# Last row blocks of an encoder layer: scalings on ScalarE and GpSimd, residual and weighting one step earlier

## The reference, cut to what matters

```python
h = _rmsnorm(x, norm_g[l]);  proj = h @ w_in[l]        # u, v, gates, q, k, v, ...
mix = jnp.concatenate([ya * silu(ga), yb * silu(gb), yc * silu(gc)], axis=-1)
x = x + jnp.einsum('bse,ed->bsd', mix, w_out[l])       # (1024, 2048)
...
y = x32 * lax.rsqrt(jnp.mean(x32 * x32, axis=-1, keepdims=True) + EPS)
return y * final_g
```

## Time and profile before

| | |
|---|---|
| median of 3 runs | 1252.67 us (1252.62 to 1253.96) |
| the profiled execution | 1252.9 us |
| its span, first to last instruction | 1251.1 us |
| granted TensorE clock | 0.997 of full speed |
| TensorE busy | 1230.0 us (98%) |
| VectorE busy | 831.2 us (66%) |
| ScalarE busy | 498.8 us (40%) |
| GpSimd busy | 54.9 us (4%) |

### The profile page before, as it was taken

One profiled execution on the slowest core, in us unless ns is written; L12 is line 12 of the kernel. 1 busy time (PEld: TensorE's weight loads), 2 busy tenths in 40 slices (PEclk: granted clock), 3 DMA queues, 4 the chain that ended last, 5 costly groups with the idle time before them and its releaser, 6 DMA issues.

```text
span 1251.1 us, 16376 instructions
## 1 busy us (share of the span) xinstructions
PE 1230.0 (98%) x6310; PEld 1014.3 (81%) x6310; DVE 831.2 (66%) x1115; ACT 498.8 (40%) x887; POOL 54.9 (4%) x70
## 2 busy tenths in 40 slices
PE   7999999999999999999999999999999999999996
PEld 6878888888988888888888887888888888888884
DVE  7657666664576577776376568777678755665556
ACT  7435454435553354454334112333333512323135
POOL 3400000003110000000000000000000000000000
PEclk9999999999999999999999999999999999999998
DMA  8499446353655256565896877659999799855769
GB/s 312 128 311 332 146 163 210 141 184 124 220 189 211 102 182 222 185 216 201 335 343 225 322 299 270 214 189 356 415 350 354 296 351 395 305 202 204 284 223 332
DMA packets 98813, 314.16 MB, mean 251 GB/s; under 512 B 10128, under 2 KB 13232, under 8 KB 87344
## 3 DMA queue, kind: packets, MB, share of 16 engines
q1 hardware_dynamic: 98736, 313.12, 69.2%
HBM read 241.77 MB, written 71.30 MB: 250 GB/s over the span
## 4 chain that ended last, share of the span: by engine, by line
PE 95%; DMA 2%; DVE 1%; ACT 1%; issue 1%; SPq 0%; ACTq 0%; DVEq 0%
PE n_bank L1561 17%; PE n_bank L1563 17%; PE n_bank L1562 17%; PE t_bank L1561 11%; PE t_bank L1562 10%; PE t_bank L1563 10%; PE e_bank L1561 2%; PE n_bank L1756 2%; PE e_bank L1563 2%; PE e_bank L1562 2%; PE n_bank L1782 2%; PE n_bank L1766 1%; DMA raw<-w_dram 1%; PE e_bank L1796 1%; PE e_bank L1806 1%
## 5 line engine op out<-in xcount | busy, mean ns | idle before, releaser
L1106 DVE TENSOR_TENSOR w_lo<-raw,w_hi 128x1024 fp32r<-128x1024 f32 (+1 forms) x116 | 138.0, 1228 | 153.2 <-ACT w_hi L812 152.9
L1561 PE MATMUL t_bank<-op_hi,w_hi 128*128 128x512 f32 x512 | 203.1, 397 | 0.0
L1562 PE MATMUL t_bank<-op_lo,w_hi 128*128 128x512 f32 x512 | 199.7, 390 | 0.0
L1563 PE MATMUL t_bank<-op_hi,w_lo 128*128 128x512 f32 x512 | 199.4, 389 | 0.0
L812 ACT ACTIVATE w_hi<-raw 128x1024 fp32r<-128x1024 f32 (+1 forms) x116 | 113.2, 1021 | 167.1 <-PE t_bank L1563 111.5
L1561 PE MATMUL n_bank<-s_ring,w_hi 128*128 128x512 f32 x448 | 178.0, 397 | 0.0
L1563 PE MATMUL n_bank<-s_ring,w_lo 128*128 128x512 f32 x448 | 174.4, 389 | 0.0
L1562 PE MATMUL n_bank<-s_ring,w_hi 128*128 128x512 f32 x448 | 174.3, 389 | 0.0
L1561 PE MATMUL n_bank<-w_hi,s_ring 128*128 128x512 f32 x448 | 174.3, 389 | 0.0
L1562 PE MATMUL n_bank<-w_lo,s_ring 128*128 128x512 f32 x448 | 174.3, 389 | 0.0
L1563 PE MATMUL n_bank<-w_hi,s_ring 128*128 128x512 f32 x448 | 174.3, 389 | 0.0
(11 more groups left out here) (225 smaller groups left out, 1825.7 us busy)
## 6 DMA issues: line engine op xcount, KB each, us to landing
s_ring<-x_parts SPq DMA_DIRECT2D x112, 512.0 KB, 6.1
s_ring<-m_parts SPq DMA_DIRECT2D x112, 512.0 KB, 6.0
raw<-w_dram SPq DMA_DIRECT2D x46, 1024.0 KB, 5.1
y_w<-w_b_dram SPq DMA_DIRECT2D x16, 1024.0 KB, 11.2
mix<-x_t_dram SPq DMA_DIRECT2D x56, 256.0 KB, 5.0
m_parts<-stage SPq DMA_DIRECT2D x24, 512.0 KB, 7.6
x_parts<-stage SPq DMA_DIRECT2D x32, 256.0 KB, 3.0
x_parts<-mix SPq DMA_DIRECT2D x32, 256.0 KB, 3.0
```

Of the source, the lines that this page charges most:

```text
L1106: ve.tensor_tensor(w_lo[:, J % 2, part], w_source(J)[:, part], w_hi[:, J % 2, part].bitcast(F32), ALU.subtract).then_inc(lo_done, 1)
L1561: pe.matmul(psum_out, stat[0], mov[0], start=first, stop=False)
L1562: pe.matmul(psum_out, stat[0], mov[1], start=False, stop=False)
L1563: return pe.matmul(psum_out, stat[1], mov[0], start=False, stop=last)
```

## The change

In the first half, y11[3] is scaled by ScalarE as a third block behind y11[2] and y12[2], and y12[3] by GpSimd; so y12[3] gets a `weigh` of its own, at step(3, 10). VectorE's part there shrinks to sum and inverse (`first_root`). In pair 3 the residual of y21[3] is added at step 12, not 13; in VectorE's program this stands ahead of `first_root`, and the last `weigh` (y22[3]) comes right behind `first_root`. In the second half GpSimd scales y22[2], ScalarE y21[2] only. In the last loop VectorE's addition of tile 3 stands ahead of its scalings of tile 2. The stores keep their order; their waits name the new semaphores.

```diff
...
         ssq_done, y_weighed, ssq_summed = sem("ssq_done"), sem("y_weighed"), sem("ssq_summed")
         y_root, y_inverted = sem("y_root"), sem("y_inverted")
         y_scaled, y_normed, y_stored = sem("y_scaled"), sem("y_normed"), sem("y_stored")
+        first_normed, second_scaled = sem("first_normed"), sem("second_scaled")
         dve_settled, pool_settled = sem("dve_settled"), sem("pool_settled")
         def w_source(J):
...
                 if n == CHUNKS - 2:
                     for c, y, done, count in ((0, y11[2], y_scaled, 4), (1, y12[2], y_scaled, 8),
-                                              (2, y11[3], y_normed, 4), (3, y12[3], y_normed, 8)):
+                                              (2, y11[3], y_scaled, 12), (3, y12[3], first_normed, 4)):
                         sp.wait_ge(done, count)
                         sp.dma_start(out[0:HS, 512 * c:512 * c + 512].rearrange("(t r) d -> r t d", t=ST), y[:]
                                      ).then_inc(y_stored, 16)
             for st in range(ST):
                 s0 = HS + P * st
-                for c, y, done, count in ((3, y22[3], y_normed, 8 + 2 * st + 1), (0, y21[2], y_scaled, 8 + 2 * st + 1),
-                                          (2, y21[3], y_normed, 8 + 2 * st + 2), (1, y22[2], y_scaled, 8 + 2 * st + 2)):
+                for c, y, done, count in ((3, y22[3], y_normed, 2 * st + 1), (0, y21[2], y_scaled, 12 + st + 1),
+                                          (2, y21[3], y_normed, 2 * st + 2), (1, y22[2], second_scaled, st + 1)):
                     sp.wait_ge(done, count)
                     sp.dma_start(out[s0:s0 + P, 512 * c:512 * c + 512], y[:, st, :]).then_inc(y_stored, 16)
             sp.wait_ge(y_stored, 16 * (4 + 4 * ST))
...
                                      sink_sb[:, 2 * (n // 2):2 * (n // 2) + 2].unsqueeze(2).broadcast_to([P, 2, 2])
                                      ).then_inc(sink_set, 1)
+            pool.wait_ge(y_inverted, 1)
+            pool.wait_ge(y_weighed, 6)
+            for st in range(ST):
+                tile = y12[3][:, st, :]
+                pool.tensor_scalar(tile, tile, rstd_y[0][:, st:st + 1], None, ALU.mult).then_inc(first_normed, 1)
+            for st in range(ST):
+                tile = y22[2][:, st, :]
+                pool.wait_ge(y_inverted, 2 + st)
+                pool.tensor_scalar(tile, tile, rstd_y[1][:, st:st + 1], None, ALU.mult).then_inc(second_scaled, 1)
         @block.scalar
         def _(sc):
...
                 sc.activation(root_y[0][:], ssq_sum[0][:], ACT.Sqrt, bias=eps_sb[:], scale=1.0 / D
                               ).then_inc(y_root, 1)
                 sc.wait_ge(y_inverted, 1)
-                for y, weighed in ((y11[2], 1), (y12[2], 2)):
+                for y, weighed in ((y11[2], 1), (y12[2], 2), (y11[3], 5)):
                     sc.wait_ge(y_weighed, weighed)
                     for st in range(ST):
                         tile = y[:, st, :]
                         sc.activation(tile, tile, ACT.Copy, scale=rstd_y[0][:, st:st + 1]).then_inc(y_scaled, 1)
-            def finish_second(st):
+            def second_root(st):
                 col = slice(st, st + 1)
                 sc.wait_ge(ssq_summed, 2 + st)
                 sc.activation(root_y[1][:, col], ssq_sum[1][:, col], ACT.Sqrt, bias=eps_sb[:], scale=1.0 / D
                               ).then_inc(y_root, 1)
+            def second_scale(st):
+                tile = y21[2][:, st, :]
                 sc.wait_ge(y_inverted, 2 + st)
                 sc.wait_ge(y_weighed, 4)
-                for y in (y21[2], y22[2]):
-                    tile = y[:, st, :]
-                    sc.activation(tile, tile, ACT.Copy, scale=rstd_y[1][:, col]).then_inc(y_scaled, 1)
+                sc.activation(tile, tile, ACT.Copy, scale=rstd_y[1][:, st:st + 1]).then_inc(y_scaled, 1)
+            def last_square(st):
+                sc.wait_ge(res_added, 6)
+                sc.wait_ge(y_added, added(PAIRS - 1, Q_A22, st))
+                square_y(1, 2, y21[3], st)
             def split_hi(J, parts=(0, 1)):
                 for part in parts:
...
                     copy_u(p, range(ST - 1))
                 if J == step(PAIR_O + 1, 12):
                     finish_first()
-            for st in range(ST):
-                sc.wait_ge(res_added, 6)
-                sc.wait_ge(y_added, added(PAIRS - 1, Q_A22, st))
-                square_y(1, 2, y21[3], st)
-                finish_second(st)
+            for st in range(ST - 2):
+                last_square(st)
+                second_root(st)
+                second_scale(st)
+            last_square(ST - 2)
+            second_root(ST - 2)
+            second_scale(ST - 2)
+            last_square(ST - 1)
+            second_root(ST - 1)
+            second_scale(ST - 1)
         @block.vector
...
             def weigh(i):
-                y, c, n = ((y11[2], 0, 1), (y12[2], 1, 2), (y22[2], 1, 3), (y21[2], 0, 4), (y11[3], 2, 5), (y22[3], 3, 7))[i]
+                y, c, n = ((y11[2], 0, 1), (y12[2], 1, 2), (y22[2], 1, 3), (y21[2], 0, 4), (y11[3], 2, 5), (y12[3], 3, 6), (y22[3], 3, 7))[i]
                 ve.wait_ge(ssq_done, ST * n)
                 ve.wait_ge(final_g_loaded, 16)
                 ve.tensor_tensor(y[:], y[:], final_g_sb[:, 512 * c:512 * c + 512].unsqueeze(1).broadcast_to([P, ST, 512]),
...
                                             ALU.subtract)
                 last.then_inc(pool_in, 1)
-            def finish_first():
+            def first_root():
                 ve.wait_ge(ssq_done, 6 * ST)
                 ve.tensor_reduce(ssq_sum[0][:], ssq[0][:], AX.X, ALU.add).then_inc(ssq_summed, 1)
                 ve.wait_ge(y_root, 1)
                 ve.reciprocal(rstd_y[0][:], root_y[0][:]).then_inc(y_inverted, 1)
-                ve.wait_ge(y_inverted, 1)
-                ve.wait_ge(y_weighed, 5)
-                for st in range(ST):
-                    tile = y11[3][:, st, :]
-                    ve.tensor_scalar(tile, tile, rstd_y[0][:, st:st + 1], None, ALU.mult).then_inc(y_normed, 1)
-                for st in range(ST):
-                    tile = y12[3][:, st, :]
-                    ve.scalar_tensor_tensor(out=tile, in0=tile, scalar=rstd_y[0][:, st:st + 1],
-                                            in1=final_g_sb[:, 1536:2048], op0=ALU.mult, op1=ALU.mult
-                                            ).then_inc(y_normed, 1)
-            def finish_second(st):
+            def second_root(st):
                 ve.wait_ge(ssq_done, 7 * ST + st + 1)
                 ve.tensor_reduce(ssq_sum[1][:, st:st + 1], ssq[1][:, st, :], AX.X, ALU.add).then_inc(ssq_summed, 1)
                 ve.wait_ge(y_root, 2 + st)
                 ve.reciprocal(rstd_y[1][:, st:st + 1], root_y[1][:, st:st + 1]).then_inc(y_inverted, 1)
+            def second_norm(st):
+                y, z = y22[3], y21[3]
                 ve.wait_ge(y_inverted, 2 + st)
-                ve.wait_ge(y_weighed, 6)
-                tile = y22[3][:, st, :]
-                ve.tensor_scalar(tile, tile, rstd_y[1][:, st:st + 1], None, ALU.mult).then_inc(y_normed, 1)
-                tile = y21[3][:, st, :]
-                ve.scalar_tensor_tensor(out=tile, in0=tile, scalar=rstd_y[1][:, st:st + 1],
+                ve.wait_ge(y_weighed, 7)
+                ve.tensor_scalar(y[:, st, :], y[:, st, :], rstd_y[1][:, st:st + 1], None, ALU.mult).then_inc(y_normed, 1)
+                ve.scalar_tensor_tensor(out=z[:, st, :], in0=z[:, st, :], scalar=rstd_y[1][:, st:st + 1],
                                         in1=final_g_sb[:, 1024:1536], op0=ALU.mult, op1=ALU.mult
                                         ).then_inc(y_normed, 1)
...
                 for t, kind, i in JOBS:
                     if t == J:
                         job(kind, i)
-                for k, t in enumerate((8, 11, 13)):
+                for k, t in enumerate((8, 11, 13 if p < PAIRS - 1 else 12)):
                     if p >= PAIR_O and j == t:
                         add_residual(p, k)
-                for i, t in enumerate((step(2, 5), step(2, 11), step(2, 13), step(3, 1), step(3, 5), step(3, 13))):
+                for i, t in enumerate((step(2, 5), step(2, 11), step(2, 13), step(3, 1), step(3, 5))):
                     if J == t:
                         weigh(i)
+                if J == step(PAIR_O + 1, 10):
+                    weigh(5)
                 if J == step(PAIR_O + 1, 12):
-                    finish_first()
+                    first_root()
+                    weigh(6)
             for st in range(ST):
                 add_chain(PAIRS - 1, Q_A22, (st,))
-                finish_second(st)
+                if st == ST - 1:
+                    second_norm(st - 1)
+                second_root(st)
+                if st != ST - 2:
+                    second_norm(st)
         @block.tensor
```

## The result

The changed kernel takes **1258.89 us** (median of 6 runs, 1258.54 to 1259.61). The kernel before, run beside it, took 1253.92 us (median of 6, 1252.62 to 1254.74). The ratio is 1.0042, 95% interval 1.0031 to 1.0052: slower by about 5 us. The profiled execution has a span of 1257.1 us, 6.0 more than the one before.

A forecast was written before the change was run, and what follows sets the result against it. The prediction took the gapless stream of stores after the first store's issue as setting the end. Span 1251.1 + 5.44 = 1256.5, with 1.8 us outside it 1258.3, for the median 1258.1 us; range 1256.6 to 1260.2.

The forecast's parts named there:

- The term that decided: Residual addition at step 12: VectorE waits for its load ahead of the sum, delaying scalings and first store by 5.44 us.
- The end is the first store plus 24.4 us: Tail: stores form one stream without a gap, so the span ends 24.4 us after the first store's issue.
- The table load at 0: ScalarE's table load before the root goes ahead of the wait, costing 0; behind it 1.28 us more, chance 0.04.
- GpSimd's tiles, taken at 1.3 us: GpSimd's four tiles of y12[3]: 1.3 us each, inside 10.9 us, term 0; GpSimd becoming the bound had chance 0.06.
- The last loop: Second half's tiles at 3.30 us each: last tiles 1.6 us or more early for the stream, term 0.
- the rule of the Trainium skill weighed in the prediction: VectorE with two SBUF inputs and GpSimd reading SBUF share an interface; fourth block ready at 1237.9, still before 1240.4.

The follow-up runs named there:

- run 1: The changed kernel with the last residual addition back at step 13, all scalings as changed: 1253.84 us against 1253.64 for the kernel before.
- Run 2: The kernel before with only the last residual addition moved to step 12: 1259.44 us against 1253.64.
- run 5: The changed kernel with GpSimd's multiplication of y12[3] done twice, same result: 1263.78 us against 1253.92 for the kernel before.
- run 3: The changed kernel with the last residual loaded at step 10 into the first weight buffer: 1254.25 us against 1253.71 for the kernel before.
- Run 4: The kernel before without the four stores of y22[2], all engine work kept: 1252.51 us against 1253.64.
- run 8: The kernel before, first half finished at step 10, two stores there, two at step 12, tile 3 added ahead of tile 2's scalings: 1250.84 us against 1253.92.
- run 6: The kernel before with the first half finished and its four stores issued at step 10, last weighting at step 12: 1255.20 us against 1253.64.

## Why the prediction was right

- **The term that decided.** Landing forecast at 1226.5 and, with the 0.80 us by which this execution was later, 1227.3; the addition started at 1227.10. Sum at 1228.85 + 0.80 = 1229.65, measured 1229.43; scalings at 1229.55 + 0.80, measured 1230.17; first store at 1232.15 + 0.80, measured 1232.76. The shift, 5.44 us forecast, was 5.26; the residual landed 8.4 us after its issue this time, and 8.4 to 9.2 in runs 1, 2 and 5, which leave its load where it was. Run 2 shows that the one line is enough for the whole loss, runs 1 and 3 that without its wait nothing of the loss remains.
- **The end is the first store plus 24.4 us.** Held to 0.1 us: 24.4 before, 24.3 after, 24.4 in runs 1, 2 and 3, and 24.3 plus the hole in run 5. Run 4 shows its limit: with one block less the chain of the tiles takes over after 1.1 of 2.8 us. The prediction had SyncE's issues wait only for room in the queue at the end. That is not quite so even in the kernel before: its issue of 1244.32 was over at 1244.97, and the next came at 1245.55, once VectorE's first scaling of the last tile (1245.04, 0.48 us) was done.
- **The table load at 0.** Right: 1223.07, ahead of the wait.
- **GpSimd's tiles, taken at 1.3 us.** Mis-sized: 1.57 us alone, 3.53 us for the first one, and the block 8.17 us:

```profile
1230.24 8.17 POOL L760 TENSOR_SCALAR mix<-mix,rstd_y 128x512 f32<-128x512 f32 x4 [652.62 <-DVE rstd_y L1389]
```

  It was covered (its store 5.7 us after the first, where 8.3 were allowed), as forecast, and run 5 shows where the cover ends.
- **The last loop.** The tile's cycle was forecast at 3.30 us and was 3.7 (1238.29 to 1242.03), since VectorE's last scaling took 1.18 instead of 0.75 us beside GpSimd. The last tile was still in time: GpSimd was done with it at 1250.7, its store was issued at 1253.12, paced by the queue; 2.4 us in hand where I had 1.6 or more. The term is 0, as forecast. The addition ahead is worth nothing here because the stream covers it; in run 8, without that cover, it showed no gain either.
- **1258.1 against 1258.89 us.** The sum started from an execution of 1252.9; over more runs the kernel before has a median of 1253.6 to 1253.9. Taken as a difference, 5.44 forecast, 5.0 measured. That the absolute numbers lie only 0.8 us apart is in part luck: the starting point was 1.25 us too low (1252.67 against 1253.92), the difference 0.5 too large.

## What to carry to other kernels

Where an engine's queue holds a step that waits for a transfer, whatever is behind it in that queue inherits the wait: before a step is moved forward, take the landing of what it needs (here 8.4 us after an issue that did not move) and compare it with the time at which the engine gets there. Where the tail is a full stream of stores, only the issue of the first one and holes behind it count; look for the earliest point at which the first block's inputs are complete, and fit its stores into the free share of the DMA engines without getting ahead of the loads that are still waited for, those of the bound engine and any other, as the residual in run 6.

## What the hardware showed that I had not expected

GpSimd's multiplication of 128x512 by a column, in the changed kernel, first tile and the two that started last in the block (by source line: ns min/median/max):

```profile
L760 POOL TENSOR_SCALAR mix<-mix,rstd_y x1: 3532/3532/3532, 1230.2 to 1230.2; 128x512 f32<-128x512 f32 x1
```

```profile
L760 POOL TENSOR_SCALAR mix<-mix,rstd_y x2: 1565/1566/1566, 1235.3 to 1236.8; 128x512 f32<-128x512 f32 x2
```

Alone it takes 1.57 us; the first, beside VectorE's weighting of 2.28 us (1230.06), took 3.53, 1.97 more, while the weighting had 2.10 us to run when the tile started at 1230.24. In run 1 VectorE's residual addition ran beside the same block as well, and the four tiles took 9.72 instead of 8.17 us:

```profile
1225.75 9.72 POOL L760 TENSOR_SCALAR mix<-mix,rstd_y 128x512 f32<-128x512 f32 x4 [647.84 <-DVE rstd_y L1389]
```

The first tile's time agrees with the rule of the Trainium skill weighed in the prediction (SBUF — State Buffer, "Who interferes with whom"): the later of the two waits out the earlier.

In the other direction the rows do not show such a wait, and the rule in these words does not fit them. VectorE's scaling with two inputs took 1.18 instead of 0.75 us in three of four tiles, and GpSimd's tile beside it 1.86 instead of 1.57, as here:

```profile
1239.07 1.86 POOL L764 TENSOR_SCALAR t<-t,rstd_y 128x512 f32<-128x512 f32 x1 [0.66 <-DVE rstd_y L1396]
```

Both became longer, and VectorE's, started later (1239.41), ended first: at 1240.59, GpSimd's at 1240.93. In the fourth case, at 1247.43, VectorE's took 0.74 us although GpSimd was also busy (from 1246.54, 1.56 us). What tells these apart was not tried.
